# The third modulation group of a two-block transformer kernel, summed along its rows by VectorE

## The reference, cut to what matters

```python
mod_x = (jax.nn.silu(c) @ w_mod[layer] + b_mod[layer])[:, None, :]
mod_c = jax.nn.silu(c_ctx) @ w_mod[layer] + b_mod[layer]
sh_m, sc_m, gt_m, sh_f, sc_f, gt_f = jnp.split(mod_x, N_MOD, axis=-1)
...
hx = modulate(rms_norm(x, g_pre_mix[layer]), sh_m, sc_m)
hc = modulate(rms_norm(ctx, g_pre_mix[layer]), csh_m, csc_m)
...
x_new = x + gt_m * rms_norm(mix_x, g_post_mix[layer])
hf = modulate(rms_norm(x_new, g_pre_ffn[layer]), sh_f, sc_f)
x_new = x_new + gt_f * rms_norm(swiglu(hf, w_ffn_in[layer], w_ffn_out[layer]), g_post_ffn[layer])
```

## Time and profile before

| | before |
|---|---|
| median of the runs | 1015.67 us |
| profiled execution | 1015.45 us |
| its span | 1013.7 us |
| TensorE busy | 995.3 us, 98% |
| VectorE busy | 584.6 us, 58% |
| ScalarE busy | 495.8 us, 49% |
| mean granted TensorE clock | 0.998 |

### The profile page before, as it was taken

One profiled execution on the slowest core, in us unless ns is written; L12 is line 12 of the kernel. 1 busy time (PEld: TensorE's weight loads), 2 busy tenths in 40 slices (PEclk: granted clock), 3 DMA queues, 4 the chain that ended last, 5 costly groups with the idle time before them and its releaser, 6 DMA issues.

```text
span 1013.7 us, 13246 instructions
## 1 busy us (share of the span) xinstructions
PE 995.3 (98%) x5164; PEld 810.6 (80%) x5164; DVE 584.6 (58%) x660; ACT 495.8 (49%) x603; POOL 0.2 (0%) x4
## 2 busy tenths in 40 slices
PE   7999999999999999999999999999999999999997
PEld 5777776778888888888888887888888878888885
DVE  5374768667555554565555665567774465555543
ACT  6473347656544443554444534663545554444432
POOL 0000000000000000000000000000000000000000
PEclk9999999999999999999999999999999999999999
DMA  9967653133655545475545465534244245555441
GB/s 373 419 272 297 274 218 126 43 121 128 213 203 173 199 169 205 166 259 174 199 166 193 166 222 182 195 125 147 102 166 166 81 147 192 198 177 202 166 166 42
DMA packets 26686, 188.32 MB, mean 186 GB/s; under 512 B 2960, under 2 KB 3216, under 8 KB 4112
## 3 DMA queue, kind: packets, MB, share of 16 engines
q1 hardware_dynamic: 26064, 185.24, 50.2%
q10 hardware_dynamic: 576, 2.43, 0.6%
HBM read 186.61 MB, written 1.05 MB: 185 GB/s over the span
## 4 chain that ended last, share of the span: by engine, by line
PE 93%; DMA 2%; DVE 2%; ACT 1%; issue 1%; SPq 1%; ACTq 0%; DVEq 0%
PE bank L1818 24%; PE bank L1820 24%; PE bank L1819 24%; DMA raw<-in_weights 2%; PE bank L2026 2%; PE bank L1862 2%; PE bank L1846 2%; PE bank L1924 2%; PE bank L1854 2%; PE bank L2292 1%; PE bank L1903 1%; PE bank L2390 1%; PE bank L2217 1%; PE bank L2168 1%; PE bank L2093 1%
## 5 line engine op out<-in xcount | busy, mean ns | idle before, releaser
L1156 DVE TENSOR_TENSOR w_lo<-raw,w_hi 128x2048 fp32r<-128x2048 f32 x148 | 338.6, 2291 | 267.6 <-ACT w_hi L641 267.4
L641 ACT ACTIVATE w_hi<-raw 128x2048 fp32r<-128x2048 f32 x148 | 283.7, 1918 | 268.1 <-PE bank L1820 217.4
L1818 PE MATMUL bank<-w_hi,hT_hi 128*128 128x512 f32 (+1 forms) x760 | 299.8, 394 | 0.0
L1820 PE MATMUL bank<-w_hi,hT_lo 128*128 128x512 f32 (+1 forms) x760 | 294.9, 388 | 0.0
L1819 PE MATMUL bank<-w_lo,hT_hi 128*128 128x512 f32 (+1 forms) x760 | 294.3, 387 | 0.0
L1818 PEld LDWEIGHTS bank<-w_hi,hT_hi 128*128 128x128 f32 x760 | 142.8, 188 | 33.0 <-issue 5.7
L1820 PEld LDWEIGHTS bank<-w_hi,hT_lo 128*128 128x128 f32 x760 | 142.7, 188 | 29.8
L1819 PEld LDWEIGHTS bank<-w_lo,hT_hi 128*128 128x128 f32 x760 | 143.0, 188 | 27.8 <-issue 0.2
L1818 PE MATMUL bank<-w_hi,gT_hi 128*128 128x512 f32 x264 | 103.4, 392 | 0.0
L1820 PE MATMUL bank<-w_hi,gT_lo 128*128 128x512 f32 x264 | 102.8, 389 | 0.0
L1819 PE MATMUL bank<-w_lo,gT_hi 128*128 128x512 f32 x264 | 102.7, 389 | 0.0
(11 more groups left out here) (310 smaller groups left out, 1008.1 us busy)
## 6 DMA issues: line engine op xcount, KB each, us to landing
raw<-in_weights SPq DMA_DIRECT2D x152, 1024.0 KB, 4.8
arena<-in_first_mods SPq DMA_DIRECT2D x8, 1024.0 KB, 14.9
memV<-in_own_mods SPq DMA_DIRECT2D x6, 1024.0 KB, 4.8
arena<-in_own_mods SPq DMA_DIRECT2D x6, 1024.0 KB, 6.9
arena<-in_const ACTq DMA_DIRECT2D x1, 1088.0 KB, 5.1
memV<-in_mem SPq DMA_DIRECT2D x1, 1024.0 KB, 6.4
x_res<-in_x SPq DMA_DIRECT2D x1, 1024.0 KB, 17.5
arena<-in_ctx SPq DMA_DIRECT2D x1, 1024.0 KB, 15.2
```

What stands on the lines that cost most here:

```text
L641: act.activation(w_hi[:, v_slot, :], raw[:, u_slot, :], ACT.Copy).then_inc(hi_ready, 1)
L1156: ins = dve.tensor_tensor(w_lo[:, v_slot, n], raw[:, u_slot, n], w_hi[:, v_slot, n].bitcast(F32), ALU.subtract)
L1818: pe.matmul(out, hi, rhi, start=start, stop=False)
L1820: return pe.matmul(out, lo, rhi, start=False, stop=stop)
```

## The change

Group 2 is taken off the products. Its eight chunks are cut into sixteen pieces of 128 rows by 1024 columns (512 KB): first the eight pieces of columns 0 to 1023, then the eight of columns 1024 to 2047. VectorE multiplies each piece by its column of silu(c) and adds it to a running total of 128 x 1024, in place in the buffer of the first piece of its half. The two totals are still to be summed over the 128 partitions: TensorE does that with four short products by ones (`mod_sums`), which put the sum into all 32 partitions of each quarter, the shape that `mod_row` had. SyncE loads the pieces into the four halves of the two `own_mods` buffers; `ROW_SLOTS` says which, and each load but the first four waits for the step that used that half before. Twelve of the loads are issued behind that of W_IN+6, four behind that of W_IN+7. The two chunks of group 2 that went through the ring are gone from it. `mod_T(1)` runs one unit earlier, behind W_IN+3, and its bank is now 7. On VectorE the block keys and decay arguments come before the low half of W_IN+5, twelve steps between the low halves of W_IN+5 and W_IN+6, the other four behind the four centrings, and `mod_columns(1)` behind these.

```diff
-VISITS = {W_IN + 2: 2, W_IN + 3: 3, W_IN + 4: 3, W_IN + 5: 3, W_IN + 6: 3, W_IN + 7: 2}
+VISITS = {W_IN + 2: 2, W_IN + 3: 3, W_IN + 4: 3}
+ROW_STEPS = 2 * MOD_K
+ROW_SLOTS = [0, 1, 2, 3, 1, 2, 3, 1, 2, 3, 1, 3, 1, 3, 1, 3]
+ROW_LOADS = {W_IN + 6: 12, W_IN + 7: 4}
...
-    plan.signalled(("modT", 1), 5)
-    plan.streamed(("mod_row", 2), 7)
+    plan.signalled(("modT", 1), 7)
+    plan.signalled(("mod_row", 2), 7)
...
+        row_mod = [mod_sum[:, e * 1024:(e + 1) * 1024] for mod_sum in own_mods for e in range(2)]
+        row_before = lambda step: max([n for n in range(step) if ROW_SLOTS[n] == ROW_SLOTS[step]], default=-1)
+        row_loads = lambda step: sum(ROW_SLOTS[n] == ROW_SLOTS[step] for n in range(step + 1))
...
+                if kind == "w" and v in ROW_LOADS:
+                    for _ in range(ROW_LOADS[v]):
+                        step = rows_in[0]
+                        rows_in[0] += 1
+                        if row_before(step) < 0:
+                            sp.wait_ge(mod_used, 2 * MOD_K)
+                        else:
+                            sp.wait_ge(sem("mod_step"), row_before(step) + 1)
+                        sp.dma_start(row_mod[ROW_SLOTS[step]], io["row_mods"][step]).then_inc(sem(f"row_loaded{ROW_SLOTS[step]}"), 16)
...
+            def mod_rows(a, b):
+                for step in range(a, b):
+                    slot, part, k = ROW_SLOTS[step], step // MOD_K, step % MOD_K
+                    total = row_mod[2 * part]
+                    dve.wait_ge(sem(f"row_loaded{slot}"), 16 * row_loads(step))
+                    if k == 0:
+                        dve.tensor_scalar(total, row_mod[slot], silu_c[:, k, 0:1], None, ALU.mult).then_inc(sem("mod_step"), 1)
+                    else:
+                        dve.wait_ge(sem("mod_step"), step)
+                        dve.scalar_tensor_tensor(out=total, in0=row_mod[slot], scalar=silu_c[:, k, 0:1], in1=total,
+                                                 op0=ALU.mult, op1=ALU.add).then_inc(sem("mod_step"), 1)
+
             low_to(W_IN + 5)
-            low_to(W_IN + 7)
             for e, part in ((0, 1), (1, 2)):
...
             ins.then_inc(sem("decay_args"), 1)
+            low_to(W_IN + 6)
+            mod_rows(0, 12)
+            low_to(W_IN + 7)
             read_out(dve, ("vr", 3))
             for tile in (2, 3):
                 centre_values(tile)
-            mod_columns(1)
             for tile in (0, 1):
                 centre_values(tile)
+            mod_rows(12, ROW_STEPS)
+            mod_columns(1)
...
-            dve.wait_ge(mod_used, N_MOD)
+            filled(dve, ("mod_row", 2))
...
+            def mod_sums():
+
+                pe.wait_ge(sem("mod_step"), ROW_STEPS)
+                b = free(pe, ("mod_row", 2))
+                for j in range(4):
+                    ins = pe.matmul(b[32 * j:32 * j + 32, :], ones[:, 0:32], row_mod[2 * (j // 2)][:, j % 2 * 512:j % 2 * 512 + 512],
+                                    start=True, stop=True)
+                ins.then_inc(full_sem(("mod_row", 2)), 1)
+
...
-                    if j == 4:
+                    if j == 3:
                         mod_T(1)
...
-                    if j < 6:
+                    if j == 2:
                         for m in mods_behind(W_IN + j + 2):
                             mod_unit(m)
+                    if j == 5:
+                        mod_sums()
                     if j == 6:
                         mod_T(2)
```

More of the change, by code:

```diff
@@ L94 @@
         _m += 1
-assert _m == N_MOD
+assert _m == N_MOD - MOD_K
 STREAM += [("w", v) for v in range(W_REG, N_W)]
-HEAD_UNITS = W_REG + N_MOD - MOD_K - len(OWN_MODS)
+HEAD_UNITS = W_REG + N_MOD - 2 * MOD_K - len(OWN_MODS)
 RAW_AT = {unit: u for u, unit in enumerate(STREAM)}
@@ L579, in mod_in @@
                 sp.dma_start(first_mod[m % len(first_mod)], io["first_mods"][m]).then_inc(sem(f"mod_loaded{m}"), 16)
+            rows_in = [0]
             sp.dma_start(cols[:], io["cols"]).then_inc(sem("cols_loaded"), 16)
@@ L722, in mod_row_out @@
             def mod_row_out(g):
-                act.wait_ge(mod_used, MOD_K * (g + 1))
+                if g == 2:
+                    filled(act, ("mod_row", 2))
+                else:
+                    act.wait_ge(mod_used, MOD_K * (g + 1))
                 if g:
@@ L2607, in lay_out @@
         "first_mods": np.stack(mods[:MOD_K]), "own_mods": np.stack([mods[m] for m in OWN_MODS]),
+        "row_mods": np.stack([f("w_mod")[0][k * P:(k + 1) * P, 2 * UNIT + c:2 * UNIT + c + 1024] for c in (0, 1024) for k in range(MOD_K)]),
         "cols": np.concatenate([small[name] for name in COLS], axis=1),
```

## The result

The changed kernel takes 1021.02 us (median of 5, 1020.26 to 1021.21), the one before 1015.08 us beside it: 1.0056 times as long, 95% interval 1.0045 to 1.0068, so 5.9 us slower. The forecast was 1017.1, with a range that ended a little over 1020.0: the direction was that of its likeliest case, the size was not. The profiled execution took 1020.26, the shortest of the five; its span is 1018.4 against 1013.7.

The account below looks back on a forecast made before the run. TensorE, 98% busy, was taken as the bound; 6.4 us net leave it, but load-paced VectorE steps leave 0.4 of that, and VectorE's lateness then makes +1.4: 1017.1 us, range from half a us below 1013.9 to a little over 1020.0.

Parts of the forecast that it names:

- its likeliest case: Row loads of 3.1 to 3.6 us make VectorE's steps late: 0 to +2.7 us on the whole kernel, chance 0.55.
- the first hole: VectorE's idle 6.85 us before the low half at 92.34, claimed to hold the 5.8 us of block keys and decay arguments.
- Rival 1: Row loads quick enough that VectorE sets the steps' pace: 4.4 us faster, 1011.3 us, chance 0.24.
- the time of a load: SyncE's 512 KB row loads: 3.35 us each, entering five times, so 0.1 us more is 0.5 us at the end.
- The four turns on the path: Slot reuses from step 1 to 11, then one for 14 and 15: 4.77 us each, load, semaphore and step included.
- what the transposes of the queries wait for: After W_IN+8, TensorE waits for VectorE's rotation instead of ScalarE's copy, going on at 152.3 against 150.91: +1.4 us.
- The 0.10 us from a landing to its step: Delay between a row load's landing and VectorE's step, 0.10 us counted in each turn of a slot.
- Rival 2: TensorE's clock falls in the new waits, losing 2.9 us: +4.3 in all, 1020.0 us, chance 0.13.

Follow-up runs that it names:

- number 7: The kernel before with only block keys and decay arguments moved ahead of the low half of W_IN+5: 1015.03 us, 0.9998 of the kernel before.
- number 2: The changed kernel with only the first four row loads issued, all sixteen steps running on those pieces: 1012.31 us, 0.9975 of the kernel before.
- number 12: The changed kernel with six loads added at a quiet time, each issued after the one before landed, to time loads alone: one execution, 1022.36 us.
- number 3: The changed kernel with each row load but the first four cut to 256 KB: 1016.18 us, 1.0012 of the kernel before.
- number 13: The changed kernel without the twelve later loads, with six more scaled additions on VectorE: 1019.90 us, 1.0053 of the kernel before.
- number 1: The changed kernel with idle products on TensorE, 18 ahead of the states and 17 ahead of the sums: 1020.95 us, 1.0062 of the kernel before.
- number 5: The changed kernel itself, unaltered, run again on another chip: 1020.83 us, 1.0052 of the kernel before.
- number 14: Number 13 plus 18 and 17 idle TensorE products ahead of the states and the sums: 1020.23 us, 1.0052 of the kernel before.
- number 6: Number 1 with the second tile of the retention's queries in bank 3 instead of bank 2: 1021.78 us, 1.0062 of the kernel before.
- number 4: The changed kernel with the sums and the rest of group 2 one unit later, behind W_IN+6: 1022.07 us, 1.0075 of the kernel before.
- number 8: The changed kernel with the last four pieces on TensorE, centrings between steps, sums later, block states read earlier: 1012.82 us, 0.9976 of the kernel before.
- number 9: Number 8 split by whole chunks, VectorE doing chunks 0 to 5 and TensorE 6 and 7: 1010.84 us, 0.9965 of the kernel before.
- number 10: The changed kernel with only the four centrings moved between steps 6 to 9, all sixteen steps kept: 1017.45 us, 1.0025 of the kernel before.
- number 11: The changed kernel with only the last four pieces given to TensorE, orders unchanged: 1019.22 us, 1.0042 of the kernel before.

## Why the prediction was wrong

**Right.** Group 2 leaves TensorE and `mod_sums` costs 1.0 to 1.1 us (0.9 forecast) at full clock. The decay arguments fit the first hole: block keys from 84.67, arguments to 90.5 (forecast 85.5 to 91.3), and number 7 shows them to be free. A scaled addition takes 1.284 us (1.28), the scaling 0.75. VectorE waits for the loads, not the reverse, and TensorE for VectorE at the states and the sums. Rival 1, VectorE setting the pace, had 1011.3; number 2, which makes it so, has 1012.3.

**The step that failed: the time of a load.** "I take 3.35, since it is the same queue, direction and row count." It was got from a load issued alone and holds for one alone (3.1 to 3.6 us, number 12). In the loop loads are in flight together, and one takes 4.3 us in the median. The first four took 0.8 us more than forecast: step 3 ends at 100.69, 9.4 behind the first issue at 91.26, forecast 8.6. The four turns on the path took 4.9, 3.5, 3.2 and 4.0 us where 3.45 stood, 1.9 more in all. That is 2.7, less the 0.7 us by which the stretch began earlier in this execution: the 2.0 us at step 15 (132.59 against 130.6). The forecast counted loads in flight together only for rival 1, as a reason for quicker ones. The page of the kernel before had the contrary:

```profile
memV<-in_own_mods SPq DMA_DIRECT2D x6, 1024.0 KB, 4.8
arena<-in_own_mods SPq DMA_DIRECT2D x6, 1024.0 KB, 6.9
```
These are the two buffers of a visit: the second load is issued 0.4 us behind the first and lands 6.9 us after its issue instead of 4.8. How much of a short load's extra time is the sharing of the engines and how much something else in the queue isn't shown. What the change adds is paid in these loads: number 2 without them is 8 us faster, number 3 with half of them 4.5, and number 13, as late by VectorE's own work, as slow.

The Trainium skill's rule to batch transfers to 1 MiB or more (DMA: Bandwidth & Descriptors, Bandwidth), which the forecast cited against the change, agrees with number 12: alone, half the bytes take two thirds to three quarters of the time (3.1 to 3.6 against 4.7 us).

**A second step: what the transposes of the queries wait for.** The forecast let VectorE's rotation release them, 21.7 us behind step 15. The rotation is over 21.2 us behind it in numbers 1, 2 and 13, and it is not what TensorE waits for: the wait there is 1.2 us in all of them, put to ScalarE's copy wherever the profile names a releaser, as before the change. The forecast had W_IN+7 start at 138 without a gate. In fact it waits for VectorE's read of the block states, 9.2 us behind step 15, and from there TensorE has 12.9 us of its own (number 1). Together that is 22.2 us from the end of step 15 to the transposes, and so it comes out in numbers 1, 2, 3 and 13. The two errors nearly cancel: 0.5 us more than the forecast's sum, partly luck.

**Small terms.** Back to back VectorE starts a step every 1.38 to 1.39 us, not 1.32, which matters only where no load is waited for (steps 12 and 13). The 0.10 us from a landing to its step stood in no row; the chain has 0.02 to 0.03.

**Rival 2 happened, and is smaller than it was priced.** From the end of the last step to the transposes it is 22.2 us where no slow product lies behind the last wait (numbers 1, 2, 3 and 13). In the changed kernel it is 23.0 (132.59 to 155.58): the sums and W_IN+6 ran at half clock, so that W_IN+7 started at 142.97, 1.1 us behind its gate. It is 23.8 in numbers 5, 12 and 14, where the clock fell behind the gate. So the clock costs 0.8 us in the first profiled execution of the changed kernel, 1.6 in the second (number 5), and 0 where another wait follows the slow products. The forecast had 2.9, the price of eight products behind the idle start. The profile grants 1.00 there; that they ran at half clock rests on their length alone, 1061 ns in the median, where the sums' took 1070 to 1090 ns at a granted 0.50.

Then the sum is 2.0 (loads) + 0.5 (gate) + 0.8 (clock) = 3.3 us above the forecast's 152.3, which is 155.6. The median of the runs is 0.8 above this execution; number 5 shows that both the loads and the clock differ from one execution to the next. In the medians the clock's share isn't resolved: 1.0056 and 1.0052 without idle products, 1.0062 with them in number 1; 1.0053 without, 1.0052 with. The idle products are no clean test either, since the clock fell all the same in numbers 6 and 14.

## What to carry to other kernels

Moving work from a full engine to one with holes is worth only what the holes' inputs arrive in time for: here the arithmetic fitted (0.9975 without the loads), the loads of 512 KB through three, then two slots did not. Time such a load as the loop will issue it, with others in flight, not alone. Look for every point at which the first engine waits for the second one's list, the release of buffers too: the first such point that binds sets the time, and here it was a bank and not the data. And where the list is late as a whole, moving one wait (number 4) or filling it (number 1) gains nothing; shorten the list, and put work without inputs of its own between the steps that wait (numbers 8 to 10).

## What the hardware showed that was not expected

- Half-filled products: in two of the four column quarters eight products of 128x512 took 3.43 us (numbers 8 and 11), in four quarters 1.72 (number 9). A quarter left empty saved nothing.
- The same wait doesn't always cost the clock. A wait of 1.9 us at W_IN+7 was followed by products at half clock in numbers 5, 12 and 14, and by none in numbers 1, 2 and 13. Of the other waits in this stretch, the nine from 3.2 to 6.4 us were all followed by a granted clock of 0.50, and so were those of 2.1 (number 6) and 2.6 us (the changed kernel), but not those of 1.6 (13), 2.0 (3), 2.4 (5) and 2.7 us (12).
- A 512 KB load takes 3.1 to 3.6 us alone, 4.3 in the loop's median and up to 6.7; with 256 KB it still takes 2.5 at least.
